# Two head pairs' scores in one group, the gating products in another bank, and a longer row of zero products at the entry

## Chip, cores and metric

The kernel runs on 1 core of one Trainium2 chip. The metric is the device time in microseconds (us). Three runs of the kernel before took 790.13, 790.6 and 791.56 us, median 790.6.

## What is computed

A trunk of two layers on 256 tokens of width 1024, in float32. Of each layer:

```
xn = rms_norm(x, norm_mix_g[l])
proj = xn @ w_in[l]                       # pool, q, k, v, gating (u, v), convolution
q, k = rope(q), rope(k)                   # 8 heads of 64
ya = pool_mixer(xa)                       # causal means over 2, 4, 8, 16 tokens, then 64x64 per group
yb = softmax(causal(q k^T / 8)) v         # 256 tokens are one block, so plain causal attention
yc = u * (tril(w_s) @ layer_norm(v) + b)  # per chunk of 128 tokens and group of 64 channels
yd = silu(layer_norm(causal depthwise conv, width 31))
x = x + (sum over branches of sigmoid(xn @ w_gate + b_gate) * (y @ w_proj)) @ w_o
x = x + (silu(g) * u) @ w_ffn_out,  g, u from rms_norm(x, norm_ffn_g[l]) @ w_ffn_in
```

A last RMS norm follows the two layers.

## The kernel before

**Units.** The weights (151 MB, each read once) pass through a ring of three 1 MB buffers, 76 units to a layer. For each unit the sync engine (SP) loads `raw`, ScalarE (ACT) rounds it to `w_hi` (`split`, L694), VectorE (DVE) takes the rest `w_lo = raw - w_hi` (L1429), and TensorE (PE) runs 48 products of 128x128 weights with 256 columns: `w_hi` by the activations' high part (L1019), `w_hi` by their low part (L1020), `w_lo` by the high part (L1021). Units 0 to 10 are the columns of `w_in` (q, q, k, k, gating v, convolution, convolution, v, v, gating u, pool), 11 to 22 gate columns, then the projections, the fourth gate, `w_o` and the feed-forward part, most of which is a loop.

**Order.** Every engine has its own program, written out by hand: a loop over the unit `u` that does the unit's work and then what `misc(l, u)` puts behind it. PE's `misc` follows the products of unit `u`. DVE's iteration is `misc(l, u)`, `merge(l, u)`, then the split of unit `u + 3`. What an engine finds in its program it does in that order, and a wait holds back all behind it.

**Banks.** PSUM has eight banks. Unit `u` writes bank `u % 4`; banks 4 to 7 take everything else. `BANKS[b]` lists the users of bank `b` in order, and `free_at(l, b, what)` turns the place in the list into the count that the semaphore `bank_free[b]` must have reached before `what` may write.

**Attention.** The scores of head pair `hp` are made after the units `ATT = (10, 12, 14, 17)`, two heads side by side in banks 4 and 5. A head uses 64 rows of the array: one product of 128 columns for the first 128 queries (L1193), one of 256 for the others (L1197). An ordinary float32 product, as these are, shows in the trace as two passes. DVE adds the causal mask and takes the maxima (L1584 to L1588, `misc(u)`), ACT the exponentials (L829), DVE the reciprocal of the sums a unit later (L1559).

**Gating.** After unit 10 (`FOLD_AT`) PE makes the products of the gating branch: eight of `zv` by `wsT` (L1209), into bank 7. DVE, at `u == FOLD_AT + 1`, adds the bias (L1593) and multiplies by `zu` (L1599), both behind the reciprocal of pair 0 and the gate factors of unit 11 (`gate_in`, L1489).

**Entry.** PE starts with 24 products of a zero matrix with itself (`warm`, L1272, 128 columns, bfloat16), turns the 16 gain rows of the first norm (L1299), turns the first two column blocks of x (`first_x(0)`, L1279, one of them a second time, L1284), and runs 8 more zero products while ACT and DVE split x and the first weight rows. Then come the first products of unit 0, and units 0 and 1 proceed by quarters as they land. The gains' copy out of the bank is L1760.

**Parameter rows.** Layer 0's per-channel parameters are loaded as 102 rows and turned by one transpose into bank 6 behind unit 4 (L1172); the 16 rows of the feed-forward norm's gain, at partition 32 of `gain_rows`, by another (L1171). The profile's name for the tile of q and k is `qk`, for banks `bank`, for `x` as loaded `gates` (the memory is shared).

Of the kernel before, what the change touches and what calls it, by code (L numbers as in the profile page):

```python
# [36 lines left out]
P = 128  # L37
# [72 lines left out]
ATT = (10, 12, 14, 17)  # L110
PV_AT = (17, 17, 21, 21)
# [5 lines left out]
def bank_users(b):  # L117
# [5 lines left out]
    users += [(POOL_AT, "pool")] if b in POOL_BANK else []  # L123
    return [what for _, what in sorted(users)] + ["A", "B", f"unit{U_GATE_D + b}"]
# [20 lines left out]
FFN_GAINS = 32  # L145
# [17 lines left out]
def build(nc, T, out, inv_freq, inv_count):  # L163
# [10 lines left out]
    with ExitStack() as ctx:  # L174
        def sb(name, shape, dt=F32):
            return ctx.enter_context(nc.sbuf_tensor(name, shape, dt))
# [69 lines left out]
        gain_rows = sb("gain_rows", [FFN_GAINS + L * KT, P])  # L246
# [348 lines left out]
        def _(pool):  # L595
# [20 lines left out]
            pool.dma_start(gain_rows[FFN_GAINS:FFN_GAINS + L * KT, :], T["norm_ffn_g"].rearrange("l (r p) -> (l r) p", p=P))\  # L616
# [65 lines left out]
        def _(act):  # L682
# [101 lines left out]
            def misc(l, u):  # L784
# [4 lines left out]
                if u == 4:  # L789
# [7 lines left out]
                    if l == 0:  # L797
                        copy(gains[:, L * KT:2 * L * KT], bank[6][:, P:P + L * KT])
# [23 lines left out]
                if u in ATT:  # L822
                    hp = ATT.index(u)
                    act.wait_ge(nmx_ready, l * HP + hp + 1)
                    for i in range(2):
                        scores = bank[4 + i][:, 0:3 * P].rearrange("p (c b k) -> p c b k", c=3, k=32)
# [4 lines left out]
                        last.then_inc(bank_free[4 + i], 1)  # L831
# [184 lines left out]
        def _(pe):  # L1016
# [148 lines left out]
            def misc(l, u):  # L1165
                if u == 4 and l == 0:
# [17 lines left out]
                if u in ATT:  # L1184

                    hp = ATT.index(u)
                    if hp == 0:
                        pe.wait_ge(rope_ready, l * 4 + 4)
                    for i in range(2):
                        bank_wait(l, 4 + i, f"S{hp}")  # L1190
                    for i in range(2):
                        h = slice(64 * i, 64 * i + 64)
                        nc.tensor.matmul(bank[4 + i][:, 0:P], qk[h, hp, 0:P], qk[h, 4 + hp, 0:P], start=True,  # L1193
                                         stop=False, skip_group_check=True)
                    for i in range(2):
                        h = slice(64 * i, 64 * i + 64)
                        nc.tensor.matmul(bank[4 + i][:, P:3 * P], qk[h, hp, P:2 * P], qk[h, 4 + hp, :],  # L1197
                                         start=False, stop=True, skip_group_check=True).then_inc(s_done, 1)
                if u == FOLD_AT:
                    bank_wait(l, 7, "F")  # L1200
# [5 lines left out]
                    for g in range(4):  # L1206
                        for t in range(TT):
                            c0 = (g // 2) * S + t * P
                            last = nc.tensor.matmul(bank[7][64 * (g % 2):64 * (g % 2) + 64, c0:c0 + P],  # L1209
# [86 lines left out]
            warm(24)  # L1296
# [688 lines left out]
```

## Time and profile before

| | |
|---|---|
| runs, median | 790.6 us |
| profiled execution | 791.62 us, its span 789.9 us |
| TensorE products busy | 783.0 us, 99% |
| VectorE | 622.1 us, 79% |
| ScalarE | 431.0 us, 55% |
| GpSimd | 150.9 us, 19% |
| DMA | 159.6 MB, 202 GB/s |

The span runs from the first to the last instruction. Busy time of PE is counted to the modelled end of each product; products overlap, so the distance between two starts is what a product costs in a row of them, and that is smaller than its duration. "Idle before" is time in which the engine did nothing, with the name of what ended it.

### The profile page before, as it was taken

What the parts mean: (1) busy time and instruction counts of PE and PEld (TensorE: products, weight loads), DVE (VectorE), ACT (ScalarE), POOL (GpSimd) and SP (SyncE); (2) the same over time, 40 slices, a digit from 0 to 9 for tenths busy, and PEclk for the clock granted to TensorE, in tenths of its full rate; (3) what the DMA queues carried; (4) which work ended last, traced back from release to release, by engine and by line L of the source; (5) the groups of instructions that cost most, each with busy time, mean ns of one, the idle gap of its engine ahead of it and who ended that gap; (6) DMA issues with size and microseconds to landing.
All of it is one profiled execution on the core that took longest, in us unless ns stands there. A gap on an engine that the chain in (4) does not pass through costs nothing.

```text
span 789.9 us, 15679 instructions
## 1 busy us (share of the span) xinstructions
PE 783.0 (99%) x6519; PEld 761.2 (96%) x6519; DVE 622.1 (79%) x771; ACT 431.0 (55%) x552; POOL 150.9 (19%) x152
## 2 busy tenths in 40 slices
PE   9999999999999999999999999999999999999997
PEld 8999999999999999999999999999999999999996
DVE  5899999976886766565698899999678767676764
ACT  6666897444654353434465578855365453444444
POOL 2405855074000000000000365623300000000000
PEclk9999999999999999999999999999999999999999
DMA  8965576767645666656568556866646466665541
GB/s 278 325 212 182 177 235 222 266 183 236 213 155 177 209 207 206 211 167 210 166 193 278 169 160 198 277 221 193 207 161 214 161 213 191 217 195 196 189 158 53
DMA packets 125388, 159.58 MB, mean 202 GB/s; under 512 B 4704, under 2 KB 107698, under 8 KB 125328
## 3 DMA queue, kind: packets, MB, share of 16 engines
q1 hardware_dynamic: 123792, 156.65, 61.1%
q0 software_dynamic: 1360, 1.82, 0.8%
q8 instruction: 43, 0.70, 0.4%
q10 hardware_dynamic: 176, 0.27, 0.1%
q14 instruction: 17, 0.14, 0.1%
HBM read 151.90 MB, written 4.72 MB: 198 GB/s over the span
## 4 chain that ended last, share of the span: by engine, by line
PE 99%; DVE 0%; ACT 0%; issue 0%; DVEq 0%; POOL 0%; ACTq 0%; POOLq 0%
PE bank L1019 28%; PE bank L1021 28%; PE bank L1020 28%; PE bank L1107 3%; PE bank L1110 3%; PE bank L1109 3%; PE bank L1079 1%; PE bank L1081 1%; PE bank L1080 1%; PE bank L1220 1%; PE bank L1067 0%; PE bank L1066 0%; PE bank L1068 0%; PE bank L1197 0%; PE bank L1193 0%; PE bank L1279 0%
## 5 line engine op out<-in xcount | busy, mean ns | idle before, releaser
L1019 PE MATMUL bank<-act,w_hi 128*128 128x256 f32 x1472 | 409.4, 278 | 0.4 <-DVE w_lo L1793 0.4
L1020 PE MATMUL bank<-act,w_hi 128*128 128x256 f32 x1472 | 407.2, 277 | 0.0
L1021 PE MATMUL bank<-act,w_lo 128*128 128x256 f32 x1472 | 407.1, 277 | 0.0
L1429 DVE TENSOR_TENSOR w_lo<-raw,w_hi 128x2048 fp32r<-128x2048 f32 x135 | 314.1, 2328 | 98.6 <-ACT w_hi L694 97.6
L694 ACT ACTIVATE w_hi<-raw 128x2048 fp32r<-128x2048 f32 (+3 forms) x146 | 265.1, 1824 | 120.3 <-PE bank L1021 86.1
L1019 PEld LDWEIGHTS bank<-act,w_hi 128*128 128x128 f32 x1472 | 277.1, 188 | 3.2 <-issue 2.7
L1020 PEld LDWEIGHTS bank<-act,w_hi 128*128 128x128 f32 x1472 | 277.0, 188 | 0.5
L1021 PEld LDWEIGHTS bank<-act,w_lo 128*128 128x128 f32 x1472 | 277.0, 188 | 0.0
L1019 PE MATMUL bank<-y_hi,w_hi 128*128 128x256 f32 x288 | 79.5, 276 | 0.0
L1020 PE MATMUL bank<-y_lo,w_hi 128*128 128x256 f32 x288 | 79.5, 276 | 0.0
L1021 PE MATMUL bank<-y_hi,w_lo 128*128 128x256 f32 x288 | 79.5, 276 | 0.0
L874 ACT ACTIVATE qk<-qk 128x512 f32<-128x512 f32 x22 | 13.9, 632 | 87.9 <-DVE qk L1489 87.9
L694 ACT ACTIVATE ff_hi<-qk 128x512 fp32r<-128x512 f32 x22 | 13.9, 633 | 81.0 <-DVE qk L1727 81.0
L632 POOL TENSOR_TENSOR conv_a<-gates,par 128x256 f32<-128x256 f32 x2 | 2.9, 1466 | 278.5 <-ACT gates L862 278.5
L1019 PEld LDWEIGHTS bank<-y_hi,w_hi 128*128 128x128 f32 x288 | 54.1, 188 | 0.0
L1020 PEld LDWEIGHTS bank<-y_lo,w_hi 128*128 128x128 f32 x288 | 54.1, 188 | 0.0
L1021 PEld LDWEIGHTS bank<-y_hi,w_lo 128*128 128x128 f32 x288 | 54.1, 188 | 0.0
L1020 PE MATMUL bank<-ff_lo,w_hi 128*128 128x256 f32 x176 | 48.7, 276 | 0.0
L1019 PE MATMUL bank<-ff_hi,w_hi 128*128 128x256 f32 x176 | 48.6, 276 | 0.0
L1021 PE MATMUL bank<-ff_hi,w_lo 128*128 128x256 f32 x176 | 48.6, 276 | 0.0
L756 ACT ACTIVATE gates<-gates,par 128x256 f32<-128x256 f32 x64 | 28.9, 502 | 26.8 <-DVE gates L1489 26.5
L636 POOL TENSOR_TENSOR conv_a<-conv_a,gates 128x256 f32<-128x256 f32 x30 | 36.2, 1207 | 20.2 <-ACT gates L862 17.4
(252 smaller groups left out, 988.9 us busy)
## 6 DMA issues: line engine op xcount, KB each, us to landing
raw<-in_w_ffn_in SPq DMA_DIRECT2D x44, 1024.0 KB, 5.1
raw<-in_w_gate SPq DMA_DIRECT2D x32, 1024.0 KB, 5.5
raw<-in_w_ffn_out SPq DMA_DIRECT2D x22, 1024.0 KB, 5.0
raw<-in_w_in SPq DMA_DIRECT2D x18, 1024.0 KB, 5.6
raw<-in_w_o SPq DMA_DIRECT2D x8, 1024.0 KB, 5.1
raw<-in_w_proj_b SPq DMA_DIRECT2D x4, 1024.0 KB, 6.1
raw<-in_w_in SPq DMA_DIRECT2D x12, 256.0 KB, 5.1
gates<-qk SPq DMA_DIRECT2D x32, 64.0 KB, 5.3
```

The costliest lines, as they stand in the source:

```text
L636: ins = nc.gpsimd.tensor_tensor(conv_a[:, 1, :], conv_a[:, 1, :], tmp, ALU.add)
L694: return nc.scalar.activation(o, i, ACT.Copy)
L756: last = nc.scalar.activation(gates[:, k, :], gates[:, k, :], ACT.Tanh, scale=0.5, bias=par[:, c:c + 1])
L874: nc.scalar.activation(ff_g, ff_g, ACT.Silu).then_inc(silu_done, 1)
L1019: nc.tensor.matmul(o, whi, ahi, start=first, stop=False, skip_group_check=skip)
L1020: nc.tensor.matmul(o, whi, alo, start=False, stop=False, skip_group_check=skip)
L1021: return nc.tensor.matmul(o, wlo, ahi, start=False, stop=last, skip_group_check=skip)
L1079: nc.tensor.matmul(o, act_hi[:, kk, ts], hi[:, k, :], start=(kk == 0), stop=False)
L1107: nc.tensor.matmul(o, y, hi[:, k, cs], start=first and k == 0, stop=False, skip_group_check=True)
L1109: nc.tensor.matmul(o, y, lo[:, k, cs], start=False, stop=False, skip_group_check=True)
L1110: last = nc.tensor.matmul(o, in_lo[:, k, ts], hi[:, k, cs], start=False, stop=last_k and k == 1, skip_group_check=True)
L1429: V.tensor_tensor(lo, raw[slot][:, :], hi.bitcast(F32), ALU.subtract).then_inc(lo_ready[slot], 1)
```

## The change

Four edits:

- Pair 1's scores are made behind pair 0's at unit 10 (`SCORES_AT`), pair 1's in banks 6 and 7 (`SCORE_BANK`). Their readers on ACT and DVE stay at their units and read those banks.
- The gating products go to bank 0 instead of 7. Its list has "F" between units 8 and 12. DVE's two additions move ahead of the reciprocal and of `gate_in`, the multiplication stays.
- The feed-forward gain rows are loaded behind the 102 parameter rows, and one transpose of 118 rows replaces two.
- At the entry the 24th zero product waits for the first x tile, the 16 gain rows are turned by an ordinary product with 128 columns of the identity, and 13 zero products follow the first transposes instead of 8.

```diff
+SCORES_AT = (10, 10, 14, 17)
+SCORE_BANK = (4, 6, 4, 4)
+FOLD_BANK = 0
...
+    users += [(FOLD_AT, "F")] if b == FOLD_BANK else []
...
-BANKS[4] = ["S0", "S1", "S2", "S3", "PV2", "C", "D", "stat2"]
-BANKS[5] = ["S0", "S1", "S2", "S3", "cT1", "C", "D"]
-BANKS[6] = ["R1", "par", "wsT", "PV3", "C", "D"]
-BANKS[7] = ["stat1", "F", "C", "D"]
+BANKS[4] = ["S0", "S2", "S3", "PV2", "C", "D", "stat2"]
+BANKS[5] = ["S0", "S2", "S3", "cT1", "C", "D"]
+BANKS[6] = ["R1", "par", "wsT", "S1", "PV3", "C", "D"]
+BANKS[7] = ["stat1", "S1", "C", "D"]
...
-            pool.dma_start(gain_rows[FFN_GAINS:FFN_GAINS + L * KT, :], T["norm_ffn_g"].rearrange("l (r p) -> (l r) p", p=P))\
+            pool.dma_start(rows[N_ROWS:N_ROWS + L * KT, :], T["norm_ffn_g"].rearrange("l (r p) -> (l r) p", p=P))\
...
-                    fg = slice(FFN_GAINS, FFN_GAINS + L * KT)
-                    nc.tensor.transpose(bank[6][:, P:P + L * KT], gain_rows[fg, :], ident[fg, fg])
-                    nc.tensor.transpose(bank[6][:, 0:N_ROWS], rows[0:N_ROWS, :], ident[0:N_ROWS, 0:N_ROWS])\
+                    both = slice(0, N_ROWS + L * KT)
+                    nc.tensor.transpose(bank[6][:, both], rows[both, :], ident[both, both])\
...
-                if u in ATT:
-
-                    hp = ATT.index(u)
+                for hp in [hp for hp in range(HP) if SCORES_AT[hp] == u]:
+                    b = SCORE_BANK[hp]
...
-                        nc.tensor.matmul(bank[4 + i][:, 0:P], qk[h, hp, 0:P], qk[h, 4 + hp, 0:P], start=True,
+                        nc.tensor.matmul(bank[b + i][:, 0:P], qk[h, hp, 0:P], qk[h, 4 + hp, 0:P], start=True,
...
                 if u == FOLD_AT:
-                    bank_wait(l, 7, "F")
+                    bank_wait(l, FOLD_BANK, "F")
...
-            warm(24)
+            warm(23)
             pe.wait_ge(pre_const, 3)
             pe.wait_ge(gain_in, 16)
-            nc.tensor.transpose(bank[0][:, 0:L * KT], gain_rows[0:L * KT, :], ident[0:L * KT, 0:L * KT])\
+            pe.wait_ge(x_in[0], 16)
+            warm(1)
+            nc.tensor.matmul(bank[0][:, 0:P], gain_rows[:, :], ident[0:L * KT, :], start=True, stop=True)\
                 .then_inc(pre_pe, 1)
             first_x(0)
-            warm(8)
+            warm(13)
...
+                if u == FOLD_AT + 1:
+
+                    dve.wait_ge(f_done, l + 1)
+                    for f in range(2):
+                        last = V.tensor_tensor(yc_f[:, f, :].rearrange("p (t s) -> p t s", t=TT),
+                                               bank[FOLD_BANK][:, f * S:(f + 1) * S].rearrange("p (t s) -> p t s", t=TT),
+                                               sgu_bias[:, f:f + 1, :].to_broadcast([P, TT, P]), ALU.add)
+                    last.then_inc(bank_free[FOLD_BANK], 1)
                 if u - 1 in ATT:
...
                 if u == FOLD_AT + 1:
 
-                    dve.wait_ge(f_done, l + 1)
-                    for f in range(2):
-                        last = V.tensor_tensor(yc_f[:, f, :].rearrange("p (t s) -> p t s", t=TT),
-                                               bank[7][:, f * S:(f + 1) * S].rearrange("p (t s) -> p t s", t=TT),
-                                               sgu_bias[:, f:f + 1, :].to_broadcast([P, TT, P]), ALU.add)
-                    last.then_inc(bank_free[7], 1)
-                    dve.wait_ge(bank_free[7], free_at(l, 7, "F", True))
+                    dve.wait_ge(bank_free[FOLD_BANK], free_at(l, FOLD_BANK, "F", True))
                     dve.wait_ge(gelu_done, l + 1)
                     V.tensor_tensor(yc_f, yc_f, zu[:, :, :], ALU.mult).then_inc(yc_ready, 1)
```

PE at the entry, before (line, operation, what it writes and reads, shape, waits):

```order
L1272 MATMUL bank<-zeros 128x128 [waits pre_const]
L1272 MATMUL bank<-zeros 128x128 x23
L1299 MATMUL bank<-ident,gain_rows 128x16 [waits gain_in,pre_const]
L1279 MATMUL bank<-ident,gates 128x128 [waits x_in0]
L1279 MATMUL bank<-ident,gates 128x128 x3
L1284 MATMUL bank<-ident,gates 128x128 x2
L1272 MATMUL bank<-zeros 128x128 x8
```

and with the change:

```order
L1274 MATMUL bank<-zeros 128x128 [waits pre_const]
L1274 MATMUL bank<-zeros 128x128 x22
L1274 MATMUL bank<-zeros 128x128 [waits x_in0,gain_in,pre_const]
L1303 MATMUL bank<-ident,gain_rows 128x128
L1281 MATMUL bank<-ident,gates 128x128 [waits x_in0]
L1281 MATMUL bank<-ident,gates 128x128 x3
L1286 MATMUL bank<-ident,gates 128x128 x2
L1274 MATMUL bank<-zeros 128x128 x13
```

The wait for the x tile stands one zero product and the gains' product earlier, and the gains' product has grown from 16 to 128 columns.

PE behind unit 10 of layer 0, with the change (before, the second group of four stood behind unit 12, with the waits on banks 4 and 5, and the gating products waited for bank 7):

```order
L1195 MATMUL bank<-qk 128x128 [waits bank_free5,bank_free4,rope_ready]
L1195 MATMUL bank<-qk 128x128
L1199 MATMUL bank<-qk 128x256 x2
L1195 MATMUL bank<-qk 128x128 [waits bank_free7,bank_free6]
L1195 MATMUL bank<-qk 128x128
L1199 MATMUL bank<-qk 128x256 x2
L1211 MATMUL bank<-wsT,gates 64x128 [waits bank_free6,vn_ready,bank_free0]
L1211 MATMUL bank<-wsT,gates 64x128 x7
```

DVE from pair 0's maxima to unit 14's split, with the change:

```order
L1602 TENSOR_SCALAR nmx<-mx 128x4
L1433 TENSOR_TENSOR w_lo<-raw,w_hi 128x2048
L1563 TENSOR_TENSOR gates<-bank,sgu_bias 128x256 x2
L1572 RECIPROCAL rden<-den 128x4
L1493 TENSOR_TENSOR gates<-bank,rms_b 128x512
L1607 TENSOR_TENSOR gates<-gates 128x512
L1513 SCALAR_TENSOR_TENSOR conv_a<-conv_h,par,conv_a 128x256 x2
L1433 TENSOR_TENSOR w_lo<-raw,w_hi 128x2048
```

Before, the additions (L1593 there) stood behind L1493's row and ahead of the multiplication; the split of unit 13 (first L1433) was and is ahead of all of them.

## Rows read from the trace of the kernel before

**Rows 1.** The page: busy us of each engine, share of the span, instructions.

```profile
PE 783.0 (99%) x6519; PEld 761.2 (96%) x6519; DVE 622.1 (79%) x771; ACT 431.0 (55%) x552; POOL 150.9 (19%) x152
```

**Rows 2.** Waits of PE over the span: us in total, times, longest.

```profile
PE bank L1272 <- POOL zeros L596: 1.1, 1, 1.1
```

**Rows 3.** Timeline of PE, entry: start us, us, engine, line, operation.

```profile
1.07 2.74 PE L1272 MATMUL bank<-zeros 128*128 128x128 bf16 x24 [1.07 <-POOL zeros L596]
3.75 0.28 PE L1299 MATMUL bank<-ident,gain_rows 16*128 16x16 f32 x1
3.96 1.11 PE L1279 MATMUL bank<-ident,gates 128*128 128x128 f32 x4
...
6.72 0.55 PE L1019 MATMUL bank<-act,w_hi 128*128 128x256 f32 x1 [0.37 <-DVE w_lo L1793]
...
9.85 0.41 PE L1020 MATMUL bank<-act,w_hi 128*128 128x256 f32 x1
10.06 0.41 PE L1021 MATMUL bank<-act,w_lo 128*128 128x256 f32 x1
...
10.47 0.28 PE L1020 MATMUL bank<-act,w_hi 128*128 128x256 f32 x1
10.59 0.28 PE L1021 MATMUL bank<-act,w_lo 128*128 128x256 f32 x1
```

**Rows 4.** Timeline of PE, end of unit 12, pair 1's scores, unit 13.

```profile
84.95 0.28 PE L1021 MATMUL bank<-act,w_lo 128*128 128x256 f32 x1
...
86.24 0.28 PE L1020 MATMUL bank<-act,w_hi 128*128 128x256 f32 x1
```

**Rows 5.** Timeline of PE behind unit 10, layer 0.

```profile
72.10 0.49 PE L1193 MATMUL bank<-qk 64*128 64x128 f32 x4
72.42 0.60 PE L1197 MATMUL bank<-qk 64*128 64x256 f32 x4
72.95 1.14 PE L1209 MATMUL bank<-wsT,gates 128*64 128x128 f32 x16
```

**Rows 6.** Timeline of DVE, units 10 and 11 of layer 0.

```profile
78.19 2.28 DVE L1429 TENSOR_TENSOR w_lo<-raw,w_hi 128x2048 fp32r<-128x2048 f32 x1
80.39 0.17 DVE L1559 RECIPROCAL rden<-den 128x4 f32<-128x4 f32 x1
...
81.05 0.74 DVE L1593 TENSOR_TENSOR gates<-bank,sgu_bias 128x256 f32<-128x256 f32 x2
...
84.21 2.82 DVE L1429 TENSOR_TENSOR w_lo<-raw,w_hi 128x2048 fp32r<-128x2048 f32 x1
```

**Rows 7.** Timeline of DVE: its last wait ahead of those rows.

```profile
26.85 0.16 DVE L1480 TENSOR_SCALAR st<-bank 128x2 f32<-128x2 f32 x1 [2.27 <-PE bank L1143]
```

**Rows 8.** Timeline, entry: ACT's first part of x, DVE's first weight row.

```profile
5.18 0.47 ACT L888 ACTIVATE act<-bank,gains 128x256 fp32r<-128x256 f32 x1 [1.68 <-PE bank L1279]
...
6.16 0.41 DVE L1793 TENSOR_TENSOR w_lo<-raw,w_hi 128x256 fp32r<-128x256 f32 x1
```

**Rows 9.** Timeline of PE: first product of unit 12, layer 0.

```profile
79.62 0.28 PE L1019 MATMUL bank<-act,w_hi 128*128 128x256 f32 x1
```

**Rows 10.** Timeline of DVE, behind unit 13's split, layer 1.

```profile
465.78 0.17 DVE L1559 RECIPROCAL rden<-den 128x4 f32<-128x4 f32 x1
```

**Rows 11.** Timeline of PE: first product of unit 12, layer 1.

```profile
466.17 0.28 PE L1019 MATMUL bank<-act,w_hi 128*128 128x256 f32 x1
```

**Rows 12.** Timeline of PE: parameter rows behind unit 4, layer 0.

```profile
38.23 0.28 PE L1068 MATMUL bank<-w_hi,act 128*128 128x256 f32 x1
...
38.60 0.31 PE L1172 MATMUL bank<-ident,rows 102*128 102x102 f32 x1
38.68 0.37 PE L1019 MATMUL bank<-act,w_hi 128*128 128x256 f32 x1
38.89 0.28 PE L1020 MATMUL bank<-act,w_hi 128*128 128x256 f32 x1
```

**Rows 13.** Loads of x (issued from 0.82 us on), us to landing.

```profile
DMA to landing us min/median/max: 2.9/4.2/5.1
```

More of the change, by code:

```diff
@@ L797, in misc @@
                     if l == 0:
-                        copy(gains[:, L * KT:2 * L * KT], bank[6][:, P:P + L * KT])
+                        copy(gains[:, L * KT:2 * L * KT], bank[6][:, N_ROWS:N_ROWS + L * KT])
                     copy(par[:, 0:r0], turned_rows[:, 0:r0])
@@ L825, in misc @@
                     for i in range(2):
-                        scores = bank[4 + i][:, 0:3 * P].rearrange("p (c b k) -> p c b k", c=3, k=32)
+                        b = SCORE_BANK[hp] + i
+                        scores = bank[b][:, 0:3 * P].rearrange("p (c b k) -> p c b k", c=3, k=32)
                         for q, cs in enumerate((slice(0, 1), slice(1, 3))):
@@ L830, in misc @@
                                                         scale=SCALE, bias=nmx[:, c:c + 1], accum_out=den[:, c:c + 1])
-                        last.then_inc(bank_free[4 + i], 1)
+                        last.then_inc(bank_free[b], 1)
                 if u - 1 in ATT:
@@ L1196, in misc @@
                         h = slice(64 * i, 64 * i + 64)
-                        nc.tensor.matmul(bank[4 + i][:, P:3 * P], qk[h, hp, P:2 * P], qk[h, 4 + hp, :],
+                        nc.tensor.matmul(bank[b + i][:, P:3 * P], qk[h, hp, P:2 * P], qk[h, 4 + hp, :],
                                          start=False, stop=True, skip_group_check=True).then_inc(s_done, 1)
                 if u == FOLD_AT:
-                    bank_wait(l, 7, "F")
+                    bank_wait(l, FOLD_BANK, "F")
                     pe.wait_ge(vn_ready, l + 1)
@@ L1208, in misc @@
                             c0 = (g // 2) * S + t * P
-                            last = nc.tensor.matmul(bank[7][64 * (g % 2):64 * (g % 2) + 64, c0:c0 + P],
+                            last = nc.tensor.matmul(bank[FOLD_BANK][64 * (g % 2):64 * (g % 2) + 64, c0:c0 + P],
                                                     zv[:, t, g * 64:(g + 1) * 64], wsT[:, g, :], start=True, stop=True)
@@ L1557, in misc @@
                     for i in range(2):
[L1558 removed]
+                        b = SCORE_BANK[hp] + i
+                        dve.wait_ge(bank_free[b], free_at(l, b, f"S{hp}", True))
                     V.reciprocal(rden[:, :], den[:, :]).then_inc(rden_ready, 1)
@@ L1582, in misc @@
                     dve.wait_ge(s_done, l * 2 * HP + 2 * hp + 2)
-                    own = banks[:, 4:6, :].rearrange("p b (q k) -> p b q k", q=2)[:, :, :, 0:P]
+                    b = SCORE_BANK[hp]
+                    own = banks[:, b:b + 2, :].rearrange("p b (q k) -> p b q k", q=2)[:, :, :, 0:P]
                     link(l, V.tensor_tensor(own, own, causal[:, :].unsqueeze(1).unsqueeze(1).to_broadcast([P, 2, 2, P]),
                                             ALU.add))
-                    V.tensor_reduce(mx[:, 0:2], banks[:, 4:6, 0:P], AX.X, ALU.max)
-                    link(l, V.tensor_reduce(mx[:, 2:4], banks[:, 4:6, P:3 * P], AX.X, ALU.max))
+                    V.tensor_reduce(mx[:, 0:2], banks[:, b:b + 2, 0:P], AX.X, ALU.max)
+                    link(l, V.tensor_reduce(mx[:, 2:4], banks[:, b:b + 2, P:3 * P], AX.X, ALU.max))
                     V.tensor_scalar(nmx[:, :], mx[:, :], -SCALE, None, ALU.mult).then_inc(nmx_ready, 1)
                 if u == FOLD_AT + 1:
-                    dve.wait_ge(f_done, l + 1)
-                    for f in range(2):
-                        last = V.tensor_tensor(yc_f[:, f, :].rearrange("p (t s) -> p t s", t=TT),
-                                               bank[7][:, f * S:(f + 1) * S].rearrange("p (t s) -> p t s", t=TT),
-                                               sgu_bias[:, f:f + 1, :].to_broadcast([P, TT, P]), ALU.add)
-                    last.then_inc(bank_free[7], 1)
-                    dve.wait_ge(bank_free[7], free_at(l, 7, "F", True))
+                    dve.wait_ge(bank_free[FOLD_BANK], free_at(l, FOLD_BANK, "F", True))
                     dve.wait_ge(gelu_done, l + 1)
```

6 lines of the change are left out of this document (2 added, 4 removed).

## Prediction, on record before the run

> **What bounds the kernel now.** I read the head of the page first: TensorE (PE) is busy for 783.0 of 789.9 us, 99% [rows 1]. The wait view says how little is left: PE waited 1.1 us for the first zeros [rows 2] and 0.37 us for the first weight rows [rows 3], and that view has no third row. So every microsecond of this kernel is an instruction of PE or the step between two of them, and a change can act in three ways only: by what PE executes, by a wait that it gives PE, and by the clock at which PE executes. No other engine's work counts unless PE comes to wait for it.
>
> The step between two products tells the clock. At 9.85 and 10.06 us products of 256 columns start 0.21 us apart, at 10.47 and 10.59 us 0.12 us [rows 3], and in unit 12 its 47 steps from 79.62 to 84.95 are 0.113 us each [rows 4, 9]: the level is 1.2 GHz up to about 10.4 us and 2.4 GHz from there. Ahead of the rise PE ran zero products, transposes and, after an idle stretch of 0.37 us, its first products.
>
> **What a comparison can tell.** The three runs of before spread over 1.4 us (790.13 to 791.56), so I take 0.2%, 1.6 us, as what can be told from no change. The profiled execution took 791.62 us, 1.0 us over the median 790.6. A microsecond of products at 1.2 GHz instead of 2.4 loses 1 - 0.113/0.213 = 0.47 us. A rise 2.1 us earlier, at about 8.3 us, would thus explain the median run; I take it so, though no row shows it. (The Trainium skill, page TensorE: Matmul & The Clock Gate, Part 1, says that the number of slow products at the start varies from run to run. One trace cannot show that.)
>
> **Scores, both layers.** Pair 1's scores leave unit 12 and follow pair 0's at unit 10, in banks 6 and 7. Alone at unit 12, from the last product at 84.95 to the second of the next unit at 86.24, they take 1.29 us; two ordinary steps would be 0.23, so the group costs 1.06 [rows 4]. Behind another pair it need not restart PE. Pair 0 shows what a pair streams: two passes of 256 columns lie between 72.42 and 72.95 [rows 5], about 0.21 each with some 0.1 for the switch, and two of 128 columns half of that, together 0.64. So it adds 0.64 at least, and 0.85 at most, which is pair 0's whole way from 72.10 to 72.95 with its switches. I take 0.66, since the step from the 128-column passes to the 256-column ones inside the group (72.10 to 72.42 for two passes) holds only one restart. Saved: 1.06 - 0.66 = 0.40 per layer, 0.80 in all (bounds 0.42 and 0.84).
>
> Against this stands a rule. The Trainium skill (same page, Part 2, step 1) lets a weight load run ahead only where row groups don't conflict or the background buffer is free; pair 1 has the row groups of pair 0. If that denied the overlap, each layer would save about 0.2 instead of 0.4, and the sum below would be +0.95 instead of +0.55. The passes inside pair 0 follow one another on the same row groups at about streaming time, which speaks for the larger value.
>
> **The gating products in bank 0: a new wait.** Bank 0 is next written by unit 12, so unit 12 can't start until VectorE (DVE) has read the eight gating products, and that is what I think decides this case. Before, they lay in bank 7, which nobody wanted for long. The change puts the two additions ahead of the reciprocal and of unit 11's gate factors, but they still stand behind the whole of unit 10's work, unit 13's split at its end. In layer 0 that split runs from 78.19 to 80.47 and the next instruction starts at 80.39 [rows 6]. DVE has not idled since 26.85 us, where it waited for PE's statistics [rows 7], so it keeps its distance to PE whatever the entry does. The two additions take 0.74 us [rows 6], so bank 0 is free at 80.39 + 0.74 = 81.13, and 0.15 us later (DVE's end at 6.57 to PE's start at 6.72 [rows 3, 8]) PE can start, at 81.28. PE reaches unit 12 at 79.62 [rows 9], later by the 0.66 of pair 1 and earlier by the 0.12 of the parameter rows below: 80.16. Idle: 1.1 us, with 0.1 for the restart 1.2. Bounds: DVE's splits take 2.28 or 2.82 us here, so 0.6 and 1.7.
>
> In layer 1 the instruction behind the same split starts at 465.78, so the additions end at 466.52 [rows 10]. PE reaches unit 12 there at 466.17 + 0.66 = 466.83 [rows 11]; with the 0.15 of the release bank 0 is ready at 466.67. No wait, by 0.16 us; upper bound 0.5 us, one long split. Put at 0.
>
> What moves back on DVE is the reciprocal and unit 11's factors, by 0.7 us; ScalarE's tanh and the scaling of pair 0 follow them, and unit 15, which needs that bank, is 15 us away. Pair 1's max at unit 12 finds its scores done. Other waits I price at nothing: banks 6 and 7 are free since unit 7 and unit 1. SP's and POOL's queues keep their order; POOL's factor DMA only has another target.
>
> **Parameter rows, layer 0.** Two transposes take 38.23 to 38.89, 0.66, of which 0.23 are ordinary steps [rows 12]. One of 118 columns saves the smaller's step, between 0.08 (38.60 to 38.68) and 0.23; I take 0.12.
>
> **The entry.** The last of the 24 zero products now waits for the first x tile. Issued at 0.8, with the shortest landing of 2.9 us [rows 13], it is there at 3.7. The 23 others, 128 columns at 1.2 GHz each, end at 1.07 + 23 x 0.107 = 3.5 [rows 3], so PE idles 0.2 to 0.3 us and runs zero product 24 at about 3.8. The gains' product (16 rows, 128 columns, real instead of transposed) is two passes of 0.21 at this clock where the transpose took one step (3.75 to 3.96). So the turned x starts at 3.8 + 0.25 + 0.43 = 4.48 instead of 3.96: 0.5 us later. ScalarE waited for just these transposes (its 1.68 us up to 5.18), DVE for it, and PE for DVE [rows 3, 8], so the first product comes at 7.25 instead of 6.72. Thirteen zero products from 5.83 last to 7.2 and fill the hole; they cost nothing, as eight plus 0.37 us of idling did. If the clock still rises at the same moment, half of that delay is made up: work that would have been done slowly is done fast. Cost: 0.5 x 0.53 = 0.27 us, bounds 0 and 0.6.
>
> **The sum.** -0.80 for scores, +1.2 for the new wait in layer 0, -0.12, +0.27: +0.55 us. On the profiled execution's 791.62 that is 792.2; on the median, 790.6, it is 791.1. All bounds at their good end give -0.5 (-0.84 + 0.6 - 0.23), at their bad end +2.3 (-0.42 + 1.7 + 0.5 - 0.08 + 0.6).
>
> **The rivals.**
> - *The clock rises earlier* (chance 0.25). For it: PE no longer idles ahead of its first product, and the new product is of the ordinary kind. Against: an idle stretch of similar length appears at 3.5 us, and the clock did not rise before 10.4 us although the engine had been busy for most of the time since 1.07. From the 8.3 us of the median run to the first product at 7.25 there is 1.05 us of slow work to save, 0.5 us, and some 0.2 where transposes run fast too: 790.4.
> - *No wait at unit 12* (0.12). If DVE got to the additions by 79.2 instead of 80.39, the 1.2 us would vanish: 789.9, and with an earlier rise 789.2. Only this with a further good bound is faster by over 0.2%. Against it stands DVE's unbroken row of work since 26.85.
> - *The entry's new wait puts the rise off* (0.13). Place: the idle stretch at 3.5 and the 0.5 us by which real products come later. Price: 0.47 us for each us of delay. 791.1 becomes slower than 792.2 from 2.3 us behind the median run's rise on, a rise after 10.6 us; one at 11.3 us gives 792.5. A late tile would do the same to a smaller degree.
> - *The pairs don't pack.* PE restarts between them: 0.4 us more, 791.5, inside the first case.
>
> **How the numbers follow.** The first case (0.50, unpacked pairs included) gives 791.1; by its bounds it could lie between 790.1 and 792.9, but they won't all fall to one side, and most of it lies between 790.4 and 791.9. With the case without the wait (789.9) and some room for its bounds below, and with the late rise (792.5) in part above, the range is 789.6 to 792.3. Faster by over 0.2% (below 789.0) takes both good rivals at once, 0.06; slower (above 792.2) is most of the late rise and the edge of the first case, 0.13; the rest, 0.81, is no difference.
>
> **What would show it.** Right: PE's wait view has a new row on DVE's additions of about 1.2 us in layer 0 and little or none in layer 1; the two groups of scores stand back to back at unit 10 within some 1.5 us, and unit 12 is followed by unit 13 at an ordinary step; x's transposes start near 4.5 us and the first product near 7.25; the step between products falls from 0.21 to 0.11 at some moment between 7 and 11 us. Wrong: no wait at unit 12 (DVE's timeline then shows how the additions got ahead), or a rise whose distance from 10.4 us outweighs everything else, times 0.47.

## The result, and the profile after

The changed kernel takes 791.98 us at the median of 22 runs (790.79 to 792.59). The kernel before, measured beside it, takes 790.26 us (22 runs, 789.67 to 791.73). The ratio is 1.0018, with a 95% interval of 1.0012 to 1.0024. By the ratio, 0.18%, this is just under the 0.2% (1.6 us) that the prediction set as the bound, and so no difference; the two medians, 1.72 us or 0.22% apart, are just over it, and the interval leaves out 1. Something did get slower. The prediction said 791.1 us, 789.6 to 792.3.

The page of the changed kernel, head and engines (profiled execution 792.05 us, so one near its median):

```profile
span 790.3 us, 15689 instructions
...
PE 782.7 (99%) x6524; PEld 761.5 (96%) x6524; DVE 621.9 (79%) x771; ACT 430.4 (54%) x552; POOL 147.9 (19%) x152
```

Five more instructions on PE than in [rows 1]: five more zero products, one more pass for the gains, one transpose less. The engine sums hardly move and tell nothing here; the waits and the steps do. The waits of PE over the span (us in total, times, longest):

```profile
PE bank L1274 <- POOL zeros L599: 1.1, 1, 1.1
PE bank L1023 <- DVE gates L1563: 0.8, 1, 0.8
PE bank L1274 <- DMA gates<-in_x: 0.3, 1, 0.3
```

The first row is that of [rows 2]. The other two are new, and both were predicted: DVE's additions at unit 12, and the first x tile. PE's timeline of the changed kernel shows three places (start us, us, engine, line, operation), first the entry:

```profile
1.07 2.63 PE L1274 MATMUL bank<-zeros 128*128 128x128 bf16 x23 [1.07 <-POOL zeros L599]
3.97 0.26 PE L1274 MATMUL bank<-zeros 128*128 128x128 bf16 x1 [0.26 <-DMA gates<-in_x]
4.16 0.79 PE L1303 MATMUL bank<-ident,gain_rows 16*128 16x128 f32 x2
4.88 1.11 PE L1281 MATMUL bank<-ident,gates 128*128 128x128 f32 x4
...
6.21 1.59 PE L1274 MATMUL bank<-zeros 128*128 128x128 bf16 x13
7.65 0.55 PE L1023 MATMUL bank<-act,w_hi 128*128 128x256 f32 x1
8.00 0.41 PE L1024 MATMUL bank<-act,w_hi 128*128 128x256 f32 x1
8.21 0.41 PE L1025 MATMUL bank<-act,w_lo 128*128 128x256 f32 x1
...
10.13 0.38 PE L1024 MATMUL bank<-act,w_hi 128*128 128x256 f32 x1
10.35 0.28 PE L1025 MATMUL bank<-act,w_lo 128*128 128x256 f32 x1
10.46 0.28 PE L1023 MATMUL bank<-act,w_hi 128*128 128x256 f32 x1
```

The gains' product holds PE for 0.72 us (4.16 to 4.88). The 13 zeros fill the hole up to the first product, which comes at 7.65. The step is 0.21 us at 8.00 and 0.11 us at 10.35: in this execution the clock is at the 1.2 GHz level for about the first 10.3 us, as in [rows 3]. Then the parameter rows of layer 0, and units 10 to 12:

```profile
38.74 0.28 PE L1072 MATMUL bank<-w_hi,act 128*128 128x256 f32 x1
38.86 0.27 PE L1175 MATMUL bank<-ident,rows 118*128 118x118 f32 x1
38.89 0.37 PE L1023 MATMUL bank<-act,w_hi 128*128 128x256 f32 x1
39.09 0.28 PE L1024 MATMUL bank<-act,w_hi 128*128 128x256 f32 x1
...
72.27 0.49 PE L1195 MATMUL bank<-qk 64*128 64x128 f32 x4
72.59 0.60 PE L1199 MATMUL bank<-qk 64*128 64x256 f32 x4
73.03 0.39 PE L1195 MATMUL bank<-qk 64*128 64x128 f32 x4
73.25 0.60 PE L1199 MATMUL bank<-qk 64*128 64x256 f32 x4
...
80.34 0.28 PE L1025 MATMUL bank<-act,w_lo 128*128 128x256 f32 x1
81.43 0.36 PE L1023 MATMUL bank<-act,w_hi 128*128 128x256 f32 x1 [0.82 <-DVE gates L1563]
81.63 0.28 PE L1024 MATMUL bank<-act,w_hi 128*128 128x256 f32 x1
```

The two pairs stand back to back. From the first one's start at 72.27 the gating products, which begin at 73.78, are 1.51 us away; before it was 0.85 [rows 5]. So pair 1 costs 0.66 here. In front of unit 12 a step that is normally 0.11 us lasts 1.09 (80.34 to 81.43). DVE's timeline of the changed kernel says what PE waited for, in layer 0 and in layer 1:

```profile
78.34 2.28 DVE L1433 TENSOR_TENSOR w_lo<-raw,w_hi 128x2048 fp32r<-128x2048 f32 x1
80.54 0.74 DVE L1563 TENSOR_TENSOR gates<-bank,sgu_bias 128x256 f32<-128x256 f32 x2
...
466.63 0.74 DVE L1563 TENSOR_TENSOR gates<-bank,sgu_bias 128x256 f32<-128x256 f32 x2
```

In layer 0 the additions end at 81.28 and PE starts at 81.43, the predicted 0.15 later. In layer 1 they end at 467.37, and PE reaches unit 12 at 467.67 (in a row not shown): no wait.

So the new waits stand where they were predicted and are about as long, and yet the kernel is 1.7 us slower instead of 0.5. The experiments are about the missing 1.2 us.

### The profile page after: what moved, and what is told of

Same layout as the page of the kernel before. It is cut to its first block, busy times and chain, and to the rows that moved or that the text cites. A ratio compares the mean times of both kernels' runs of the same rounds, so it can differ in the third digit from the quotient of the medians.

```text
span 790.3 us, 15689 instructions
## 1 busy us (share of the span) xinstructions
PE 782.7 (99%) x6524; PEld 761.5 (96%) x6524; DVE 621.9 (79%) x771; ACT 430.4 (54%) x552; POOL 147.9 (19%) x152
## 4 chain that ended last, share of the span: by engine, by line
PE 92%; DVE 6%; issue 1%; DMA 0%; ACT 0%; DVEq 0%
PE bank L1023 27%; PE bank L1025 26%; PE bank L1024 26%; DVE w_lo L1433 3%; PE bank L1111 3%; PE bank L1114 3%; PE bank L1113 3%; PE bank L1222 1%; PE bank L1084 0%; PE bank L1083 0%; PE bank L1085 0%; DMA gates<-in_x 0%; PE bank L1281 0%; PE bank L1199 0%; DVE gates L1538 0%
## 5 line engine op out<-in xcount | busy, mean ns | idle before, releaser
L1433 DVE TENSOR_TENSOR w_lo<-raw,w_hi 128x2048 fp32r<-128x2048 f32 x135 | 314.3, 2330 | 98.7 <-ACT w_hi L697 97.7
L680 POOL TENSOR_TENSOR gates<-gates,qk 128x512 f32<-128x512 f32 x16 | 28.5, 1809 | 58.9 <-DVE qk L1661 58.9
```

What stands on the lines that cost most here:

```text
L680: nc.gpsimd.tensor_tensor(m, m, mtmp[:, i % 2, :], ALU.add).then_inc(madd_done, 1)
L1433: V.tensor_tensor(lo, raw[slot][:, :], hi.bitcast(F32), ALU.subtract).then_inc(lo_ready[slot], 1)
```

## The experiments

All were run 11 times, four kernels to a chip on three chips, with 33 runs of the kernel before beside each four. Its median was 790.19, 790.16 and 790.16 us there, so differences of medians can be read against 790.2. Two theories opened the study. Theory 1: the entry made the loss, and the units' parts cancel (in its sharp form, the idle stretch at 3.5 us keeps the clock down). Theory 2: the wait at unit 12 made it, by more than its own length. A third came out of the first four kernels. Theory 3: the gains' product takes away a rise of the clock that the kernel before has in most of its runs, ahead of its first product. Its rival is named in the expectations as Theory 4.

### Parts alone: the units, the entry, its wait, and another bank

**The units' part alone** is the change with the entry of before:

```diff
-            warm(23)
+            warm(24)
...
-            pe.wait_ge(x_in[0], 16)
-            warm(1)
-            nc.tensor.matmul(bank[0][:, 0:P], gain_rows[:, :], ident[0:L * KT, :], start=True, stop=True)\
+            nc.tensor.transpose(bank[0][:, 0:L * KT], gain_rows[0:L * KT, :], ident[0:L * KT, 0:L * KT])\
...
-            warm(13)
+            warm(8)
```

> The change without its entry edits (24 zero products, transposed gains, 8 zero products as before); scores, gating bank, additions' place and parameter rows as in the change. Theory 1 (the entry made the loss, the units' parts cancel): -0.80 for scores, -0.22 for the parameter rows, +1.06 for the wait at unit 12 give +0.0 us: same time as before within 0.3 us, and a spread of runs like that of before. Theory 2 (the wait at unit 12 and what follows it made the loss): +1.0 us or more against before.

Measured: 790.34 us (789.92 to 791.58), ratio 1.0001 [0.9991, 1.001], or +0.15 us. It has the wait at unit 12 and still costs next to nothing, so Theory 2 falls. PE's timeline of this kernel, in an execution of 790.12 us, is the key to the case:

```profile
3.74 0.28 PE L1301 MATMUL bank<-ident,gain_rows 16*128 16x16 f32 x1
3.96 1.11 PE L1281 MATMUL bank<-ident,gates 128*128 128x128 f32 x4
...
5.29 1.06 PE L1274 MATMUL bank<-zeros 128*128 128x128 bf16 x8
6.72 0.35 PE L1023 MATMUL bank<-act,w_hi 128*128 128x256 f32 x1 [0.37 <-DVE w_lo L1799]
6.91 0.28 PE L1024 MATMUL bank<-act,w_hi 128*128 128x256 f32 x1
7.03 0.28 PE L1025 MATMUL bank<-act,w_lo 128*128 128x256 f32 x1
```

Its entry is that of before instruction for instruction, and starts its first product at the same 6.72 us as [rows 3]. But the step behind it is already 0.12 us. The clock was at 2.4 GHz before the first product. The eight zeros still took 1.06 us, as at 1.2 GHz, so it rose at their end or in the idle stretch behind them. The row of [rows 7] shows what that is worth. The same place in DVE's timeline, units alone:

```profile
25.34 0.16 DVE L1482 TENSOR_SCALAR st<-bank 128x2 f32<-128x2 f32 x1 [0.40 <-PE bank L1147]
```

25.34 against 26.85 before: 1.5 us, and the two executions are 1.50 us apart too (790.12 and 791.62). It is so in the other profiled executions: from the start of this row on, the nine kernels with the units of before take 764.76 to 764.80 us each (791.62 - 26.85 = 764.77 in before itself), but for one at 764.89. So what an execution loses at its entry is lost by this row. The three kernels with the change's units and bank 0 take 764.69 to 764.78.

The runs of before bear out that it has two kinds of execution. Of the 33 beside each four kernels, 6, 6 and 7 lie at 791.5 to 791.7 us, and all others between 789.6 and 790.9, none in between. The profiled execution of before, 791.62 us, was one of the few whose rise came late; its median run has it early. (The Trainium skill, page TensorE: Matmul & The Clock Gate, Part 1, says that the number of slow products at the start varies from run to run. These runs agree: one kernel falls into two groups, 1.4 us apart.)

**The entry alone** is the kernel before with the three edits of the entry (23 zeros, the wait for x and one more; the gains by an ordinary product; 13 zeros instead of 8):

```diff
-            warm(24)
+            warm(23)
...
-            nc.tensor.transpose(bank[0][:, 0:L * KT], gain_rows[0:L * KT, :], ident[0:L * KT, 0:L * KT])\
+            pe.wait_ge(x_in[0], 16)
+            warm(1)
+            nc.tensor.matmul(bank[0][:, 0:P], gain_rows[0:L * KT, :], ident[0:L * KT, :], start=True, stop=True)\
...
-            warm(8)
+            warm(13)
```

> The kernel before with the three entry edits alone. Theory 1: +1.4 us against before (the whole difference), first product near 7.6 us, no wait at unit 12. Theory 2: at most +0.5 us, the later start with half of it made up.

Measured: 791.73 us (790.15 to 792.51), ratio 1.0014 [1.0005, 1.0023], +1.54 us. Here is the loss. Three of its 11 runs are below 790.7, eight above 791.2. PE's timeline of this kernel, in an execution of the median's 791.73 us:

```profile
7.51 0.55 PE L1019 MATMUL bank<-act,w_hi 128*128 128x256 f32 x1
...
8.93 0.75 PE L1279 MATMUL bank<-ident,gates 128*128 128x128 f32 x4
...
9.64 0.28 PE L1020 MATMUL bank<-act,w_hi 128*128 128x256 f32 x1
9.76 0.28 PE L1021 MATMUL bank<-act,w_lo 128*128 128x256 f32 x1
```

The first product comes 0.79 us later than before, and the clock rises within the transposes at 8.93 (0.75 us; in the other timelines, in rows not shown, these four take 1.05 or 1.06 at 1.2 GHz and 0.60 at 2.4). So the entry loses twice: by a later first product, and by the products behind it that run slowly.

**The wait alone:** before, with the 24th zero product behind the wait for x.

```diff
-            warm(24)
+            warm(23)
...
+            pe.wait_ge(x_in[0], 16)
+            warm(1)
```

> The kernel before with one edit: the 24th zero product waits for the first x tile (23 + 1 zero products), transposed gains and 8 zero products as before. Theory 1 in its sharp form (the idle stretch at 3.5 us keeps the clock from rising ahead of the first products): +0.8 to +1.3 us, although the first product comes only 0.2 to 0.4 us later, and runs spread over 1.5 us or more. Rival (only the later start counts): +0.1 to +0.4 us, spread as before.

Measured: 790.38 us (789.8 to 791.91), ratio 0.9998 [0.9989, 1.0007], +0.19 us; in its profile the products start at 6.99 us with steps of 0.20 and 0.12. One of its 11 runs, 791.91, is late, as some of before's are. The idle stretch does not keep the clock down, and the sharp form of Theory 1 falls. With it falls the prediction's own rival, the entry's new wait putting the rise off.

**Bank 1 for the gating products:** the units' part alone, with one number changed.

```diff
-FOLD_BANK = 0
+FOLD_BANK = 1
```

> As the first (the change without its entry edits), but with the gating products in bank 1, which unit 13 wants, not unit 12. Bank 1 is read out from 72.0 to 72.7 us, ahead of the gating products, and wanted again at about 85 us, after the additions at 80.4 to 81.1. Both theories: no wait at unit 12, so -0.80 - 0.22 = -1.0 us against before, 789.2 us, below both kernels. If it is not faster by at least 0.7 us, the wait was not what unit 12's 1.06 us were.

Measured: 789.0 us (788.93 to 790.47), ratio 0.9987 [0.9978, 0.9996], -1.2 us, and 1.34 us below the units' part with bank 0. Bank 1 is next written by unit 13, so there are some 5 us more. The waits of PE in this kernel:

```profile
PE bank L1274 <- POOL zeros L599: 1.1, 1, 1.1
PE bank L1023 <- DVE w_lo L1799: 1.0, 1, 1.0
```

None is on L1561, the additions. (The second row is at the first product, where PE idled 0.37 us in [rows 3]. In this execution the clock rose ahead of the zeros, and they ended sooner.) Two of its 11 runs, 790.4 and 790.47, are late by the same 1.4 us as before's. The wait at unit 12 was therefore real and cost about what the trace said (1.34 us by the medians, 1.19 between the two profiled executions behind DVE's row, 764.78 against 763.59), and the grouping of the scores pays when the bank is free.

### What in the entry costs

**The product alone:** before, with only the gains' transpose turned into an ordinary product of 16 rows and 128 columns.

```diff
-            nc.tensor.transpose(bank[0][:, 0:L * KT], gain_rows[0:L * KT, :], ident[0:L * KT, 0:L * KT])\
+            nc.tensor.matmul(bank[0][:, 0:P], gain_rows[0:L * KT, :], ident[0:L * KT, :], start=True, stop=True)\
```

> The kernel before with one edit: the gain rows are turned by the ordinary product of 16 rows and 128 columns (no wait for x ahead of it, 24 and 8 zero products). Theory 3 (the wait alone cost 0.2 us and left the clock's early rise, so the gains' product is what took it away): +1.0 to +1.5 us, hardly a run below 790.3, the rise after the first product in the profile. Theory 4 (no single edit, the sum of later starts does it): +0.3 to +0.6 us with the early rise kept in most runs.

Measured: 791.25 us (789.95 to 791.98), ratio 1.0011 [1.0002, 1.0021], +1.09 us. This single line carries most of the loss. Two of its 11 runs are at 789.95 and 790.18, the other nine at 791.09 or above. The rise behind the first product that was expected of the profile isn't in it: the profiled execution happens to be the one of 790.18 us, and PE's timeline there shows the clock up early all the same:

```profile
3.74 0.79 PE L1299 MATMUL bank<-ident,gain_rows 16*128 16x128 f32 x2
4.46 0.67 PE L1279 MATMUL bank<-ident,gates 128*128 128x128 f32 x4
...
6.78 0.36 PE L1019 MATMUL bank<-act,w_hi 128*128 128x256 f32 x1 [0.98 <-DVE w_lo L1793]
6.98 0.28 PE L1020 MATMUL bank<-act,w_hi 128*128 128x256 f32 x1
```

The four transposes take 0.67 us instead of 1.11, so the rise fell within them and the first product came at 6.78, hardly later than before. The product's own length costs almost nothing there; what it costs is that such an execution becomes rare. That the other nine had the late rise is read from their times: with the clock up and the first product later by the whole 0.50 us (4.46 against 3.96) they would take 790.12 + 0.50 = 790.62, and the fastest of them took 0.47 us more. The late rise itself is seen in the entry alone, above, and in the wait with the product, below.

**The zeros alone:** before, with 13 instead of 8.

```diff
-            warm(8)
+            warm(13)
```

> The kernel before with one edit: 13 zero products ahead of the first product instead of 8. Theory 3: no loss where the clock is at 1.2 GHz; where it rose early the zeros are short and hide in the wait for DVE; 0.0 us in the median, and fewer runs at 791.5 to 791.7 if the idle 0.37 us is what puts the rise off there. If the zeros were to blame for the change's loss: +1 us.

Measured: 790.29 us (789.84 to 790.98), ratio 0.9998 [0.9989, 1.0007]. No change at the median, and no run above 791. In its profiled execution (789.84 us) the clock rose already within the first transposes, and the first product comes 0.27 us earlier than before:

```profile
3.96 0.85 PE L1279 MATMUL bank<-ident,gates 128*128 128x128 f32 x4
...
6.45 0.36 PE L1019 MATMUL bank<-act,w_hi 128*128 128x256 f32 x1 [0.70 <-DVE w_lo L1793]
```

**The wait and the zeros, without the product:**

```diff
-            warm(24)
+            warm(23)
...
+            pe.wait_ge(x_in[0], 16)
+            warm(1)
...
-            warm(8)
+            warm(13)
```

> The kernel before with the wait for x ahead of the 24th zero product and 13 zero products behind, gains transposed as before: the change's entry without its product. Theory 3: as the wait alone, +0.2 us, early rise in most runs. Theory 4: +0.5 us or more with runs spread evenly.

Measured: 790.48 us (790.31 to 790.61), ratio 0.9999 [0.999, 1.0008], +0.32 us. It is the entry alone without the product, and 1.25 us under it. This too has no late run: with 13 zeros and a transpose, 22 of 22 runs are below 791, where about one in six of before's is not.

**The wait and the product, with 8 zeros:**

```diff
-            warm(24)
+            warm(23)
...
-            nc.tensor.transpose(bank[0][:, 0:L * KT], gain_rows[0:L * KT, :], ident[0:L * KT, 0:L * KT])\
+            pe.wait_ge(x_in[0], 16)
+            warm(1)
+            nc.tensor.matmul(bank[0][:, 0:P], gain_rows[0:L * KT, :], ident[0:L * KT, :], start=True, stop=True)\
```

> The kernel before with the wait and the product, 8 zero products: the change's entry without its five more zeros. Theory 3: +1.4 us or somewhat more, like the whole entry. Rival (zeros and product together): +0.5 us.

Measured: 791.74 us (791.39 to 792.59), ratio 1.0016 [1.0007, 1.0025], +1.58 us. Not one run is early: with the first product at 7.50 instead of 6.72 and the clock up, one would take 790.12 + 0.78 = 790.90, and the fastest took 791.39. PE's timeline of this kernel (792.04 us):

```profile
4.02 0.79 PE L1301 MATMUL bank<-ident,gain_rows 16*128 16x128 f32 x2
...
7.50 0.55 PE L1019 MATMUL bank<-act,w_hi 128*128 128x256 f32 x1 [0.37 <-DVE w_lo L1795]
...
9.99 0.32 PE L1020 MATMUL bank<-act,w_hi 128*128 128x256 f32 x1
10.15 0.28 PE L1021 MATMUL bank<-act,w_lo 128*128 128x256 f32 x1
```

The rise comes at 10 us, 3.3 us or more behind that of the units alone, most of it spent on products at half speed. From the wait alone to the wait with the product the median rises by 1.36 us. The two profiled executions are 1.59 us apart; 0.51 of it is the later first product (7.50 against 6.99), the rest products at 1.2 GHz.

### The kind of instruction, or any later start?

A product that takes 0.5 us more could also do harm by its length. Two kernels put other work there. Neither leaves out anything; the added results aren't used.

**Transposes as filler:** the gains' transpose made four times.

```diff
+            for _ in range(3):
+                nc.tensor.transpose(bank[0][:, 0:L * KT], gain_rows[0:L * KT, :], ident[0:L * KT, 0:L * KT])
             nc.tensor.transpose(bank[0][:, 0:L * KT], gain_rows[0:L * KT, :], ident[0:L * KT, 0:L * KT])\
```

> The kernel before with the gains' transpose made four times over (the same result into the same place), which puts off the x transposes about as long as the ordinary product does, 0.6 us, with no ordinary product. Theory 3a (the kind of instruction took the early rise away): about +0.6 us at most, early rise in most runs. Theory 3b (any 0.5 us ahead of the transposes does): +1.1 to +1.5 us, as with the product.

Measured: 790.46 us (790.11 to 791.71), ratio 1.0002 [0.9993, 1.0012], +0.30 us, with two runs above 791 (791.03 and 791.71). It is a weaker test than was meant: in its profile the x transposes start at 4.28, 0.32 us later than before and not 0.6, where the product puts them off by 0.50.

**A product of full rows:** one ordinary product of the identity with itself behind the gains' transpose.

```diff
+            nc.tensor.matmul(bank[3][:, 0:P], ident[:, :], ident[:, :], start=True, stop=True)
```

> The kernel before with one ordinary float32 product more, identity by identity (128 rows, 128 columns, result unused), behind the gains' transpose. If an ordinary product of 16 rows is what the clock takes for idling, full rows do no harm: +0.3 to +0.6 us for the later start, most runs early. If an ordinary float32 product as such, or its 0.5 us, does it: +1.1 to +1.5 us.

Measured: 790.67 us (789.99 to 790.92), ratio 0.9998 [0.9989, 1.0007], +0.51 us, no late run. PE's timeline of this kernel (790.71 us):

```profile
4.03 0.80 PE L1301 MATMUL bank<-ident 128*128 128x128 f32 x2
4.61 1.06 PE L1279 MATMUL bank<-ident,gates 128*128 128x128 f32 x4
...
7.32 0.36 PE L1019 MATMUL bank<-act,w_hi 128*128 128x256 f32 x1 [0.94 <-DVE w_lo L1794]
7.51 0.28 PE L1020 MATMUL bank<-act,w_hi 128*128 128x256 f32 x1
```

Its x transposes start at 4.61, 0.65 us later than before and later than in the kernel with the product alone, its first product comes at 7.32, and the clock is up all the same. So neither the delay nor an ordinary product as such takes the early rise away. What is left is something about the gains' product. In both kernels the identity is what streams; of the gains' product only its first 16 rows do, so 112 of the 128 columns are all zero, and the weights that it streams past are the gains instead of the identity. The two products also differ in that one replaces the gains' transpose and the other follows it, and in the bank that they write (0 and 3). Rows, values and these weren't separated.

**The change without its product:** every other part of the change stays.

```diff
-            nc.tensor.matmul(bank[0][:, 0:P], gain_rows[:, :], ident[0:L * KT, :], start=True, stop=True)\
+            nc.tensor.transpose(bank[0][:, 0:L * KT], gain_rows[0:L * KT, :], ident[0:L * KT, 0:L * KT])\
```

> The change with one edit undone: the gain rows are transposed again (16 columns) instead of multiplied; wait, 13 zeros, scores and gating bank stay. Theory 3: the units' parts cancel (+0.0), the wait costs 0.2 to 0.3: 790.4 us against before's 790.2, all runs close together. If the product is not the cause within the whole change: 791.5 us or more.

Measured: 790.38 us (789.88 to 791.21), ratio 1.0 [0.9991, 1.0009]: 1.60 us below the change, and equal to before. The runs are not as close together as was expected; the highest, 791.21, is the profiled one, and the clock is up early in it too. The last section comes back to it.

### A version that beats both

**Bank 1 with 13 zeros:** the bank 1 kernel with the longer filler, meant to take away its late runs.

```diff
-            warm(8)
+            warm(13)
```

> The version with gating products in bank 1 and before's entry, with 13 zero products instead of 8. The gating products' wait is gone as in that version (789.0 us), and if the idle 0.37 us ahead of the first product is what puts the clock's rise off in about one run in six of before, no run falls near 790.4 to 790.5 us as two of eleven did: 789.0 us, all runs below 789.9. If the zeros do nothing: the same median and one or two late runs.

Measured: 789.27 us (788.71 to 790.46), ratio 0.9985 [0.9976, 0.9994]. The expectation that all runs fall below 789.9 missed by one, 790.46, and it isn't better than bank 1 alone (789.0), though its lowest run is. The best kernel of the study is thus the units' part with bank 1 and the old entry: 1.2 us under before, 3 us under the change.

## Why the prediction was right or wrong

The range holds, and so, by the ratio, does the verdict, but partly by luck: the median moved by 1.72 us where 0.55 was forecast, the likeliest time, 791.1, is 0.9 us low, and the reason for most of the loss is another than the one given. The range reached so far in part because it had room for a late rise that was put down to something else, and the median of before that it starts from, 790.6, is 0.34 us above that of 22 runs. Point by point:

- **Scores, -0.80: right.** Pair 1 costs 0.66 behind pair 0, so 0.40 a layer is saved. The Trainium skill's rule about row groups (TensorE: Matmul & The Clock Gate, Part 2, step 1), read so that only 0.2 would have been left, does not show: pair 1's passes follow on pair 0's rows at streaming time. (Where the prediction speaks of two passes of 256 and two of 128 columns, [rows 5] has four of each, two to a product. Its times, 0.21 us and half of that, are those of the products, so the 0.64 stands.)
- **The wait at unit 12, +1.2: right.** The step into the unit lasts 1.09 instead of 0.11, and the next one 0.20, so it costs 1.06. Bank 1 brought 1.34. Layer 1 has none, as said: PE comes 0.30 us behind the end of the additions, 0.15 of it for the release, where 0.31 and 0.16 were predicted.
- **Parameter rows, -0.12: too small.** From the last product ahead of them to the second of the next unit it was 0.66 us [rows 12] and is 0.35 (38.74 to 39.09). So 0.31 is saved: the two transposes had a step of 0.21 ahead of them, 0.16 between them and 0.08 behind (their rows start at 38.44, not shown, and 38.60).
- **The units together.** Predicted +0.28, by the rows -0.80 + 1.06 - 0.31 = -0.05, measured +0.15, all within what can be told. Behind DVE's row of [rows 7], where the entry no longer varies, the three executions with these units take 764.78, 764.69 and 764.72 us against 764.77.
- **The entry, +0.27 with bounds 0 and 0.6: this step failed on the median.** Alone it measured +1.54. Between the two profiled executions, both with a rise at about 10.4 us, it holds: the first product comes 0.93 us later (7.65 against 6.72; 0.53 was predicted, but the product started at 4.16 instead of 4.05 and took 0.72 us instead of 0.43), and at DVE's wait, 27.36 (in a row not shown) against 26.85 [rows 7], 0.51 is left, so about half was indeed made up. With the units' -0.05 that gives 0.46, and the executions lie 792.05 - 791.62 = 0.43 apart, against the predicted 0.55. The condition, "if the clock still rises at the same moment", is what the usual run doesn't meet.
- **Beneath it lies the reading of the median.** "A rise 2.1 us earlier, at about 8.3 us, would thus explain the median run; I take it so, though no row shows it." The formula of 0.47 us for each us holds only while real products run slowly. The three runs that were given, 790.13, 790.6 and 791.56, were, by their times, two groups and not a spread: one rise at 10.4 us and two ahead of the first product, at 6.72. A still earlier one gains little (0.27 us in the profile of the zeros alone), and there is 1.5 us to lose. Nor is half of a delay made up where the clock is up already: the product of full rows put the first product off by 0.60 us and lost 0.61 at DVE's row. The case "the clock rises earlier" (0.25) could not pay for the median run, which had it already.
- **The rival with the late rise (0.13, 792.5) described the outcome but not the cause.** In the change's profiled execution, which is at its median, the rise comes behind the first product, and this decided the result. It need not be so in every run: with the first product at 7.65 and the clock up, one would take about 25.34 + 0.93 + 764.69 = 790.96, and the fastest of the 22 took 790.79, the next 791.18. But it was the gains' product (+1.09 alone, -1.60 when undone in the change), and not the wait (+0.19).

By the medians: +0.15 from the units, 0.2 from the wait and the later start, about 1.4 from the product, in sum 1.75; measured 1.72. Of what the entry's part is made can be read from the profiled executions (us; "DVE's row" is the start of the one of [rows 7] in each kernel, most of them in rows not shown):

| kernel | first product | from it to DVE's row | DVE's row |
|---|---|---|---|
| units alone, clock up early | 6.72 | 18.62 | 25.34 |
| wait alone, up early | 6.99 | 18.68 | 25.67 |
| product of full rows, up early | 7.32 | 18.63 | 25.95 |
| before, the late kind | 6.72 | 20.13 | 26.85 |
| entry alone | 7.51 | 19.42 | 26.93 |
| wait and product | 7.50 | 19.75 | 27.25 |
| the change | 7.65 | 19.71 | 27.36 |

The third column is the same where the clock is up at the first product, and longer by the work done at 1.2 GHz where it isn't. The change's execution is 2.02 us behind that of the units alone: 0.93 because its first product comes later, 1.09 because the products behind it are slow. So the late rise is about half of what the entry does, and the plain delay, which the prediction had halved, the other half. The product has a share in both.

What stays open: why the clock rises late in most runs with the gains' product, by its rows, its values or something else; and why 13 zeros seem to take away the late runs only where the gains are transposed (none in the 22 runs above; whether the 790.46 of bank 1 with 13 zeros is one isn't known). The change with transposed gains, bank 1 and its wait for x wasn't run; the nearest is bank 1 with 13 zeros.

## What to carry to other kernels

Where a time hangs on an event that varies from run to run, such as the rise of the clock at the start, first ask whether the runs form groups and which of them the profiled execution belongs to: a profile of the rarer group hides what the usual run has to lose. Count the filler ahead of the first real product as part of the kernel: replacing one small transpose by an equivalent product cost 1.4 us, twelve products of the main loop. And when a result moves into another bank, read who writes that bank next and when: one bank further on, the same regrouping turned from +0.15 into -1.2 us.

## What the runs showed of the hardware

- The clock can be up before the first real product with nothing behind it but zero products (bf16, all zero) and f32 transposes: steps of 0.12 us from 6.91 us on in the units' part alone. With an ordinary product of 16 rows in place of one transpose, 9 of 11 runs lost this, by their times.
- The profile's column of the granted clock does not show the level there. The table by stretches of the kernel before (us, PE busy, clock, DMA share, GB/s) prints 1.00 for a stretch in which the steps are 0.21 us [rows 3], so the steps between equal products have to be read:

```profile
7.00:10.30 3.30, 3.30 (x17) 1.00 1.00 339
```

- One idle stretch of 0.61 us stands in the profile of bank 1 with 13 zeros, with no releaser, and one of 0.77 us at 20.39 in that of the change without its product. PE's timeline of the former:

```profile
20.15 0.35 PE L1023 MATMUL bank<-act,w_hi 128*128 128x256 f32 x1 [0.61 <-issue]
```

No other engine or transfer is named, and nothing was tried on it. Between 11 and 30 us none of the other 12 profiles has such a row; these two kernels share the units' part, 13 zeros and an early rise. The execution with bank 1 took 789.82 us, 0.89 more than that of bank 1 with 8 zeros, and 0.88 of it is there at DVE's row (26.22 against 25.34), so the stretch is the greater part of its loss; the other, at 791.21, is the slowest of its 11. It may be why 13 zeros didn't improve the median with bank 1; this is argued, not shown.
